# A hybrid decoder layer on one core: the mask of the forgetting attention moves from TensorE to GpSimd, its tiles run in the opposite order, and one product of the last expert turn changes places on VectorE

## The chip, the core and the metric

The kernel runs on one core of one Trainium2 chip. The core has five engines that take their instructions in order and wait for each other on semaphores: TensorE (PE, matrix products into PSUM), VectorE (DVE), ScalarE (ACT), GpSimd (POOL) and SyncE (SP, which here only issues DMAs). The metric is the device time of one execution in microseconds (us). Lower is better.

## The reference, cut to what matters

512 tokens of 1024 channels go through one layer: four token mixers with gates (a short convolution, a stick-breaking attention, a forgetting attention, a convolution module), then a mixture of 32 experts, then a final RMSNorm. Both attentions have four heads of 64 channels and are causal.

```python
# stick-breaking attention, per head
z = q @ k.T * scale
mask = kpos < qpos
log_not = where(mask, log_sigmoid(-z), 0)
after = reverse_cumsum(log_not) - log_not
out = where(mask, exp(log_sigmoid(z) + after), 0) @ v

# forgetting attention, per head; dcum is a running sum over the tokens of log forget gates
logits = q @ k.T * scale + dq[:, None] - dcum[None, :]
logits = where(kpos <= qpos, logits, -inf)
out = softmax(logits) @ v

# experts: each token takes two of 32
out += combine[:, e] * ((silu(t @ w_gate[e]) * (t @ w_up[e])) @ w_down[e])
```

## The kernel before

The program is written by hand, one instruction stream for each engine. The order of work is the order in which it is written; there is no scheduler. It has these stages, by the trace of before: eleven projections of the normalised input (to about 136 us), sixteen attention steps (144 to 295 us), the rest of the gates and branch products (to about 400 us), the output projection and the router, and then 17 expert turns to the end. Expert weights stream in by DMA through a ring of 21 buffers.

**The attention steps** (the tensor block's loop over `n in range(STEPS + 1)`, STEPS = 16, four steps for each head). One step does one tile of each attention:

- Of the stick-breaking attention, `stick_step(n)` gives key tile `kt = 3 - n % 4`. Its scores are keys x queries and cover the columns `q0:` = `kt * 128` to 512, so 128, 256, 384 and 512 columns in the four steps of a head.
- Of the forgetting attention, `fox_step(n)` gives query tile `qt = n % 4`. Its scores are queries x keys and cover the columns `0:m`, `m = (qt + 1) * 128`: also 128, 256, 384 and 512 columns. `fox_head` takes the other head of the same pair, which lies in the other 64 partitions.

In a step TensorE runs, in this order:

1. three pairs of score products, of the stick-breaking one into bank 0 (L1904) and the forgetting one into bank 1 (L1905). Both contract over 64 partitions, one in the lower and one in the upper half of the array's rows;
2. two 128x128 products that add a mask to the diagonal blocks: `identb` x `cutb` into bank 0 (L1906, after it `z_psum` is raised) and `identb` x `maskb` into bank 1 (L1908, after it `l_psum`);
3. 24 products of 512 columns for the gates (L1848, in the last steps L1873);
4. the running sums of the stick-breaking attention (L1915, L1918);
5. the products of weights and values of step n - 1: stick-breaking (L1927, output of 64 partitions and 512 - q0 columns, written before the other in the program) and forgetting (L1932, one product of 128 columns for each pair of key tile and query tile, so qt + 1 of them, output in the other 64 partitions). Both are plain float32 and appear in the trace as two records for each product;
6. the transposes of the forgetting weights (L1939, qt + 1 of them), and six branch products (L1860).

Meanwhile VectorE takes bank 0 (L1276, waits for `z_psum`), subtracts `dcum` from bank 1 with a running maximum (L1283, waits for `l_psum`, then raises `l_max`), and makes the split parts that TensorE's step 4 waits for (`spl`, L1108). ScalarE does the exponentials, among them `wts` (L958) and `pt` (L963), which step 5 of the next round waits for. GpSimd only adds up `run` (L694 to L697). `dcum`, the running sums broadcast to all partitions, has come by DMA before the first step.

**The last expert turn** (turn 16, `LAST`). TensorE multiplies the gate weights and then the up weights with the tokens (L2175), VectorE makes `hid` = gate and up product (L1105, raises `hid_r`), TensorE transposes it (L2184) and multiplies it with the down weights (L2201). While that goes on the results of the earlier turns, scattered to `y_dram`, are loaded back as four tiles of 128 tokens. `gather_results(1, tiles)` on VectorE waits until a tile has landed and adds its two weighted rows to the token (two instructions, L1105). Tile 1 (`EARLY_ROWS`) is loaded first; tiles 2 and 3 (`LATE_ROWS`) are weighted after the last turn, and TensorE takes tile 0. Then come the final norms and the stores.

VectorE's order in the last turn before:

```python
for j in range(2): dve.tensor_scalar(cw_diag[:, j, :], ...)
gather_results(1, EARLY_ROWS)
dve.wait_ge(S["silu"], E + 1)
dve.wait_ge(S["gu_done"], E + 1)
stt(hid[:, :], ...).then_inc(S["hid_r"], 1)
```

Of the kernel before, what the change touches and what calls it, by code (L numbers as in the profile page):

```python
# [48 lines left out]
def hybrid_trunk(nc, x, mix_norm_g, w_in, b_forget, conv_a_w, conf_dw_w, conf_dw_b, conf_ln_g,  # L49
                 conf_ln_b, w_branch, w_gate, b_gate, w_out, ffn_norm_g, w_router_group,  # L50
                 w_router_expert, w_expert_gate, w_expert_up, w_expert_down, final_norm_g, out):
    P = 128
# [50 lines left out]
    with main:  # L103
# [6 lines left out]
        def sem(name):  # L110
# [15 lines left out]
        rv = sb(main, "rv", [NT, 2, NE], F32R)  # L126
        neg_tri = sb(main, "neg_tri", [P], F32R)
        neg_one = sb(main, "neg_one", [P], F32R)
        maskb = sb(main, "maskb", [P], BF16)
        strictb = sb(main, "strictb", [P], BF16)  # L130
        oneb = sb(main, "oneb", [P], BF16)
        eps = sb(main, "eps", [1])
# [169 lines left out]


        S = {name: sem(name) for name in (
            "pool_step act_step dve_step consts small_in tabs_ready x0 x1 x2s x3 sq_done root xn_ready "
            "xt_psum hi_out xt_ready raw0 raw1 rest0 rest1 hi_ready split_ready unit_used "
            "tabs_psum free_p0 free_p1 "
            "ln_in ln_sum ln_cent ln_sq ln_root ln_norm ln_act y_ready ya ya_hi ya_split bf_in ff_step "
# [78 lines left out]
            return i // PER * PER + (i + 1) % PER  # L387

        def fox_step(n):
            return fox_head(n // NT), n % NT, (n % NT + 1) * P  # L390

        def x_tile(n):

# [251 lines left out]
        def _(pool):  # L645
# [5 lines left out]
                                          pattern=[[step, cols]], channel_multiplier=mult)  # L651

            for t, v in ((ident, 0.0), (causal, 1.0), (tri_made, -1.0), (one_made, -1.0),
                         (maskb, 0.0), (cutb, 0.0), (strictb, 1.0), (oneb, 1.0), (eps, EPS)):
                st.mark(pool.memset(t[:], v))
            st.mark(pool.memset(cu[:, :, 0:CF_W - 1], 0.0))
            st.mark(pool.memset(ca[:, :, 0:CA_W - 1], 0.0))
# [4 lines left out]
            st.mark(select(ident, P, ALU.not_equal, 1.0, 0, -1, 1))  # L662
            st.mark(select(causal, T, ALU.is_ge, 0.0, 0, 1, -1))
            st.mark(select(tri_made, P, ALU.is_ge, 0.0, 0, -1, 1))
            st.mark(select(maskb, P, ALU.is_ge, MASKED, 0, -1, 1))
            st.mark(select(cutb, P, ALU.is_gt, MASKED, 0, 1, -1))
            st.mark(select(strictb, P, ALU.is_gt, 0.0, 0, 1, -1))
            st.done()
            st.link(pool.tensor_copy(identb[:, :], ident[:, :]))
            pool.sem_inc(S["consts"], 1)  # L670

            evacuated(pool, "ac")
            evacuated(pool, "ab")
# [8 lines left out]
            for j in range(BJ):  # L682
                pool.wait_ge(S["ya_hi"], j + 1)
                pool.tensor_tensor(yl[0][:, j, :], axb[:, j, :], yh[0][:, j, :].bitcast(F32), ALU.subtract).then_inc(S["ya_split"], 1)

            for n in range(STEPS):
                h, kt, q0 = stick_step(n)
                if kt == 0:
                    continue
                pool.wait_ge(S["sp_max"], n + 1)  # L690
                if n:
                    pool.wait_ge(S["sp_lo"], parts(n))
                if kt == NT - 1:
                    pool.tensor_copy(run[:, q0:], sp[:, q0:]).then_inc(S["run_ready"], 1)  # L694
                else:
                    st.link(pool.tensor_copy(run[:, q0:q0 + P], sp[:, q0:q0 + P]))
                    pool.tensor_tensor(run[:, q0 + P:], run[:, q0 + P:], sp[:, q0 + P:], ALU.add).then_inc(S["run_ready"], 1)  # L697
# [96 lines left out]
        def _(act):  # L794
# [9 lines left out]
            for t in range(NT):  # L804
                act.wait_ge(x_in[t], 16)
                act.activation(junk[:, :], xt[:, t, :], ACT.Square, accum_out=stat[:, 0, t:t + 1]).then_inc(S["sq_done"], 1)
                act.wait_ge(S["sq_done"], t + 1)
                if t == 0:
                    act.wait_ge(S["consts"], 1)
                act.activation(stat[:, 1, t:t + 1], stat[:, 0, t:t + 1], ACT.Sqrt, bias=eps[:, 0:1], scale=1.0 / D).then_inc(S["root"], 1)  # L810

            def first_hi(part):
# [288 lines left out]
        def _(dve):  # L1101
# [75 lines left out]
                        st.mark(stt(sg[:, j, :], win, ch[:, j, CA_W + i:CA_W + i + 1], sg[:, j, :], ALU.mult, ALU.add))  # L1177

            split_lo(1, KC * PROJ[1][2])
            dve.wait_ge(S["consts"], 1)  # L1180
            st.mark(dve.tensor_copy(causal_r[:, :], causal[:, :]))
            st.mark(dve.tensor_copy(neg_tri[:, :], tri_made[:, :]))
            st.mark(dve.tensor_copy(neg_one[:, :], one_made[:, :]))
# [87 lines left out]
            for n in range(STEPS + 1):  # L1271
                if n < STEPS:

                    h, kt, q0 = stick_step(n)
                    dve.wait_ge(S["z_psum"], n + 1)
                    dve.tensor_scalar(tmp[:, q0:], bank[0][:, q0:], CAP, None, ALU.min).then_inc(S["sp_min"], 1)  # L1276

                    h, qt, m = fox_step(n)
                    sm = small[:, n % 2, :]
                    dve.wait_ge(S["l_psum"], n + 1)  # L1280
                    if n >= 1:
                        dve.wait_ge(S["pt_psum"], n)
                    st.link(dve.tensor_tensor_reduce(out=lg[:, 0:m], in0=bank[1][:, 0:m], in1=dcum[:, h, 0:m], scale=1.0,  # L1283
                                                     scalar=-3e38, op0=ALU.subtract, op1=ALU.max, accum_out=sm[:, 0:1]))
                    dve.sem_inc(S["l_max"], 1)

                    st.link(dve.tensor_tensor(sm[:, 1:2], sm[:, 0:1], dq[:, qt, h:h + 1], ALU.add))
                    dve.tensor_tensor(sm[:, 2:3], dq[:, qt, h:h + 1], sm[:, 1:2], ALU.subtract).then_inc(S["l_bias"], 1)

                    g, d = x_tile(n)  # L1290
                    b, c = gp[:, n % 2, :], gs[:, n % 2, :]
                    dve.wait_ge(S["xg_neg"], n + 1)
                    dve.tensor_scalar(b, c, CAP, None, ALU.min).then_inc(S["xg_min"], 1)
                    h, kt, q0 = stick_step(n)
                    dve.wait_ge(S["sp_ln"], n + 1)
                    if n:
                        dve.wait_ge(S["run_ready"], runs(n))
                    stt(sp[:, q0:], bank[0][:, q0:], 0.0, tmp[:, q0:], ALU.add, ALU.max).then_inc(S["sp_max"], 1)
                    dve.wait_ge(S["l_exp"], n + 1)
                    st.link(dve.reciprocal(sm[:, 4:5], sm[:, 3:4]))  # L1300
                    dve.tensor_scalar(lg[:, 0:m], lg[:, 0:m], sm[:, 4:5], None, ALU.mult).then_inc(S["l_norm"], 1)
                    dve.wait_ge(S["sp_hi"], parts(n) + 1)
                    if n:
                        dve.wait_ge(S["acc_done"], n)
                    lo(spl[:, q0:], sp[:, q0:], sph[:, q0:]).then_inc(S["sp_lo"], 1)
                    dve.wait_ge(S["xg_ln"], n + 1)
                    dve.tensor_tensor(b, b, c, ALU.max).then_inc(S["xg_max"], 1)
                    k, part = (n + 3) // 2, (n + 1) % 2
                    if n >= 1 and k <= NX:
                        x_lo_part(k, part)  # L1310

                    dve.wait_ge(S["xg_exp"], n + 1)
                    dve.wait_ge(S["xb_ps"], n + 1)
                    if g == 0:
                        dve.tensor_tensor(hsum[:, :, d, :], by_tile(c), by_tile(bank[4 + n % 2][:, :]), ALU.mult).then_inc(S["xg_free"], 1)
                    else:
                        dve.tensor_tensor(b, c, bank[4 + n % 2][:, :], ALU.mult).then_inc(S["xg_free"], 1)
                        dve.wait_ge(S["xg_free"], n + 1)
                        dve.tensor_tensor(hsum[:, :, d, :], hsum[:, :, d, :], by_tile(b), ALU.add)
                    if kt:  # L1320
                        dve.wait_ge(S["sp_hi"], parts(n) + 2)
                        lo(run_l[:, q0:], run[:, q0:], run_h[:, q0:]).then_inc(S["sp_lo"], 1)
                    if n == STEPS - 1:
                        gate_lo(1, 1)
# [288 lines left out]
            def expert_pass(c):  # L1613
# [16 lines left out]
                for i in range(turns):  # L1630
# [10 lines left out]
                    if isinstance(c, int) and i == LAST:  # L1641
                        dve.wait_ge(S["flag_ready"], 1)
                        most.append(dve.value_load(flag[0:1, 0:1], min_val=0, max_val=T))
                        for j in range(2):
                            dve.tensor_scalar(cw_diag[:, j, :], ident[:, :], cw[:, j, 0:1], None, ALU.mult).then_inc(S["comb"], 1)
                        gather_results(1, EARLY_ROWS)
                    dve.wait_ge(S["silu"], E + 1)
                    dve.wait_ge(S["gu_done"], E + 1)
                    stt(hid[:, :], bank[3][:, 0:FE], rslot[:, column(c, i)], act_g[:, :], ALU.mult, ALU.mult).then_inc(S["hid_r"], 1)
                    if i + 1 < turns:  # L1650
                        for b in range(2):
                            x_out(E + 1, b)
# [89 lines left out]
        def _(pe):  # L1742
# [9 lines left out]
            pe.wait_ge(S["dve_step"], 1)  # L1752
            for n in range(NIDLE):
                nc.tensor.matmul(bank[3][:, 0:P], pt[:, 0, :], pt[:, 1, :], start=True, stop=True)
            pe.wait_ge(S["consts"], 1)

            for t in range(NT):
                pe.wait_ge(S["xn_ready"], t + 1)
# [135 lines left out]
            for n in range(STEPS + 1):  # L1894
                if n < STEPS:
# [6 lines left out]
                    j2, r2 = head_rows(h)  # L1902
                    for i, (kz, qz, ql, kl) in enumerate(((k_s, q_s, q_f, k_f), (k_s, q_sl, q_f, k_fl), (k_sl, q_s, q_fl, k_f))):
                        nc.tensor.matmul(bank[0][:, q0:], kz[r:r + HD, j, kt * P:(kt + 1) * P], qz[r:r + HD, j, q0:], start=i == 0, stop=i == 2)  # L1904
                        nc.tensor.matmul(bank[1][:, 0:m], ql[r2:r2 + HD, j2, qt * P:(qt + 1) * P], kl[r2:r2 + HD, j2, 0:m], start=i == 0, stop=i == 2)  # L1905
                    nc.tensor.matmul(bank[0][:, q0:q0 + P], identb[:, :], cutb[:, :], start=False, stop=True,  # L1906
                                     skip_group_check=True).then_inc(S["z_psum"], 1)
                    nc.tensor.matmul(bank[1][:, m - P:m], identb[:, :], maskb[:, :], start=False, stop=True,  # L1908
                                     skip_group_check=True).then_inc(S["l_psum"], 1)
                    gates(BEHIND_SCORES)  # L1910
                if n < STEPS:
                    h, kt, q0 = stick_step(n)
# [336 lines left out]
```

## Time and profile before

| | |
|---|---|
| median of 3 runs | 710.95 us (710.42 to 713.12) |
| the profiled execution | 711.37 us, of it 709.5 us are the span of the profile |
| TensorE busy | 690.8 us (97%) |
| VectorE busy | 373.2 us (53%) |
| ScalarE busy | 254.5 us (36%) |
| GpSimd busy | 91.3 us (13%) |
| mean rate of the DMAs | 232 GB/s |
| chain that ended last | PE 89%, DVE 4%, DMA 3%, ACT 1% |

The span is the time from the first to the last record of the profile. Busy is the time in which at least one instruction of an engine ran. The last line follows the execution back from its last instruction, at each step to what released it. Matmuls overlap, their starts are recorded and their ends are modelled: the time that a group of them costs is read from start to start.

### The profile page before, as it was taken

The page shows a single profiled execution, that of the slowest core. Times are in us where ns is not written, and L with a number is a line of the kernel's source. Part 1 is how long each engine was busy: PE and PEld are TensorE (multiplying, and loading weights), DVE is VectorE, ACT ScalarE, POOL GpSimd, SP SyncE. Part 2 cuts the span into 40 slices and gives each one's busy share as a digit, 9 for nine tenths or more (in the row PEclk, how much of TensorE's full clock was granted, in tenths as well). Part 3 has the DMA queues.
Part 4 walks back from the last instruction along what each step waited for, and adds up shares of the span by engine and source line. Part 5 has one row for each costly group of instructions (what it writes and reads, how often), then busy time and mean ns, then how long its engine had stood idle before and what let it go on. Part 6 is the DMA issues. An engine that isn't in the chain of part 4 may idle for free.

```text
span 709.5 us, 10025 instructions
## 1 busy us (share of the span) xinstructions
PE 690.8 (97%) x3923; PEld 508.0 (72%) x3923; DVE 373.2 (53%) x732; ACT 254.5 (36%) x423; POOL 91.3 (13%) x130
## 2 busy tenths in 40 slices
PE   8999999999999999999999999999999999999894
PEld 7888988777777777788888888666555556555442
DVE  5378996666676868556446214752513121212227
ACT  7332133587676777544244211220101111111113
POOL 2000922000000101100003000011311312131100
PEclk9999999999999999999999999999999999999998
DMA  7523244322222111493406699699999999999993
GB/s 241 177 61 118 61 127 143 139 75 75 75 75 74 48 59 49 162 385 113 136 2 237 225 382 346 268 353 387 405 417 420 403 419 418 419 419 417 419 394 134
DMA packets 60585, 164.58 MB, mean 232 GB/s; under 512 B 8090, under 2 KB 39911, under 8 KB 48116
## 3 DMA queue, kind: packets, MB, share of 16 engines
q1 hardware_dynamic: 54820, 151.77, 56.3%
q0 software_dynamic: 5712, 12.11, 4.6%
q8 instruction: 33, 0.54, 0.3%
q14 instruction: 20, 0.16, 0.1%
HBM read 155.68 MB, written 16.00 MB: 242 GB/s over the span
## 4 chain that ended last, share of the span: by engine, by line
PE 89%; DVE 4%; DMA 3%; ACT 1%; issue 1%; POOL 0%; SPq 0%; POOLq 0%; DVEq 0%; ACTq 0%
PE psum L1749 31%; PE psum L2175 14%; PE psum L1848 12%; PE psum L2201 8%; PE psum L2028 6%; PE psum L1860 3%; PE psum L2141 2%; DVE ring_e L1105 2%; DMA ring_e<-y_dram 2%; PE psum L1873 1%; PE psum L1904 1%; PE psum L2184 1%; DMA y_dram<-ye,slots_b 1%; PE psum L1987 1%; PE psum L1939 1%
## 5 line engine op out<-in xcount | busy, mean ns | idle before, releaser
L1749 PE MATMUL psum<-xh,wh 128*128 128x512 f32 x256 | 99.9, 390 | 0.8 <-DVE xl L1105 0.8
L1749 PE MATMUL psum<-xl,wh 128*128 128x512 f32 x256 | 99.6, 389 | 0.0
L1749 PE MATMUL psum<-xh,wl 128*128 128x512 f32 x256 | 99.6, 389 | 0.0
L1108 DVE TENSOR_TENSOR wl<-raw,wh 128x1280 fp32r<-128x1280 f32 (+4 forms) x37 | 71.8, 1945 | 24.6 <-ACT wh L801 9.0
L1105 DVE SCALAR_TENSOR_TENSOR hid<-psum,rslot,act_g 128x256 f32<-128x256 f32 x17 | 8.2, 483 | 92.3 <-PE psum L2175 91.7
L1749 PEld LDWEIGHTS psum<-xh,wh 128*128 128x128 f32 x256 | 48.1, 188 | 11.0 <-DVE xl L1105 1.0
L1749 PEld LDWEIGHTS psum<-xh,wl 128*128 128x128 f32 x256 | 48.1, 188 | 10.0
L1749 PEld LDWEIGHTS psum<-xl,wh 128*128 128x128 f32 x256 | 48.1, 188 | 9.8
L1848 PE MATMUL psum<-xh,wh 128*128 128x512 f32 x128 | 51.3, 401 | 0.0
L1848 PE MATMUL psum<-xh,wl 128*128 128x512 f32 x128 | 50.1, 391 | 0.0
L1848 PE MATMUL psum<-xl,wh 128*128 128x512 f32 x128 | 49.9, 390 | 0.0
L1105 DVE SCALAR_TENSOR_TENSOR sg<-cu,ch,sg 128x512 f32<-128x512 f32 x60 | 48.7, 882 | 0.0
L2175 PE MATMUL psum<-ring_w,xT 128*64 128x256 f32 x256 | 38.8, 383 | 0.0
L1054 ACT ACTIVATE act_g<-psum,rslot 128x256 f32<-128x256 f32 x17 | 8.0, 473 | 77.7 <-PE psum L2175 49.3
L1056 ACT ACTIVATE hidT<-psum 128x256 f32<-128x256 f32 x17 | 6.5, 383 | 78.2 <-PE psum L2184 78.2
L1670 DVE COPY ye<-psum 128x512 f32<-128x512 f32 x15 | 10.4, 691 | 44.2 <-PE psum L2201 44.2
L739 POOL DMA_INDIRECT y_dram<-ye,slots x15 | 13.7, 913 | 143.8 <-DVE ye L1670 125.4
L1335 DVE TENSOR_TENSOR gp<-gs,psum 128x512 f32<-128x512 f32 x16 | 11.0, 685 | 36.8 <-PE psum L1749 36.0
L2175 PEld LDWEIGHTS psum<-ring_w,xT 128*64 128x64 f32 x256 | 22.3, 136 | 10.5 <-issue 3.4
L976 ACT ACTIVATE gs<-psum,bg 128x512 f32<-128x512 f32 x16 | 10.9, 687 | 50.2 <-PE psum L1749 50.2
L1848 PEld LDWEIGHTS psum<-xh,wl 128*128 128x128 f32 x128 | 24.0, 188 | 5.2
L1848 PEld LDWEIGHTS psum<-xl,wh 128*128 128x128 f32 x128 | 24.1, 188 | 4.6
(388 smaller groups left out, 1531.6 us busy)
## 6 DMA issues: line engine op xcount, KB each, us to landing
raw<-in_w_gate SPq DMA_DIRECT2D x16, 1024.0 KB, 6.3
raw<-in_w_in SPq DMA_DIRECT2D x9, 1024.0 KB, 5.5
ring_w<-in_w_expert_gate SPq DMA_DIRECT2D x8, 1024.0 KB
ring_w<-in_w_expert_up SPq DMA_DIRECT2D x8, 1024.0 KB
ring_h<-in_w_expert_down SPq DMA_DIRECT2D x8, 1024.0 KB
ring_h<-in_w_expert_gate SPq DMA_DIRECT2D x6, 1024.0 KB
ring_e<-in_w_expert_down SPq DMA_DIRECT2D x6, 1024.0 KB
ring_e<-in_w_expert_gate SPq DMA_DIRECT2D x6, 1024.0 KB
```

Source lines behind the costliest of these rows:

```text
L739: pool.indirect_dma_start(out=y_dram[:, :], out_offset=bass.IndirectOffsetOnAxis(ap=slots[first, p], axis=0), in_=ye[first, :], in_offset= ...
L976: act.activation(gs[:, m, :], gate_bank(cg, m)[:, :], ACT.Sigmoid, bias=bg[:, d:d + 1]).then_inc(S["gate_mul"], 1)
L1105: return dve.scalar_tensor_tensor(out=out_, in0=a, scalar=s, in1=b, op0=o0, op1=o1)
L1108: return dve.tensor_tensor(dst, src, hi.bitcast(F32), ALU.subtract)
L1335: dve.tensor_tensor(gp[:, m, :], gs[:, m, :], branch_bank(cg, m)[:, :], ALU.mult).then_inc(S["gate_free"], 1)
L1749: last = nc.tensor.matmul(dst, a, b, start=start and n == 0, stop=stop and n == len(seq) - 1)
L1848: last = nc.tensor.matmul(bank[6 + n % 2][:, :], a[:, c, f], b[:, c, :], start=c == 0 and q == 0, stop=c == KC - 1 and q == 2)
L1860: last = nc.tensor.matmul(bank[4 + n % 2][:, :], a[:, j, f], b[g][:, j, :], start=j == 0 and q == 0, stop=j == BJ - 1 and q == 2)
L2028: last = nc.tensor.matmul(bank[t][:, :], x_[:, t, c, :], w_[:, b, c, :], start=c == 0 and m == 0, stop=c == KC - 1 and m == 2)
L2141: last = nc.tensor.transpose(bank[b][:, (k % 4) * P:(k % 4 + 1) * P], xg[:, s, :].rearrange("p (n c) -> p c n", c=KC)[:, k, :], ident[:, :])
L2175: last = nc.tensor.matmul(dst[half, 0:FE], xT[:, k, half], w[h][:, k, :], start=k == 0, stop=k == KC - 1)
L2201: last = nc.tensor.matmul(bank[5 + b][half, :], hidT[:, m, half], w_d[h][:, m, b * T:(b + 1) * T], start=m == 0, stop=m == FE // P - 1)
```

## The change

There are two parts, and each one moves something.

**The mask.** `maskb`, its memset, its select and TensorE's sixteen products with it (L1908) are gone. GpSimd writes the mask into `dcum` itself: `later_keys(n)` selects over the 128 columns of the diagonal block of head h and puts +2^100 where the key lies after the query, so that VectorE's subtraction (L1283) gives the masked logit. One block of `dcum` is read by all later query tiles too, so the mask may only go in when they are done: `fox_step` now takes the query tiles from the last to the first (`qt = 3 - n % 4`, so m = 512, 384, 256, 128 in the steps of a head), and GpSimd masks the block of step n + 1 after VectorE has raised `l_max` for step n. VectorE waits for this mask (`made`) ahead of L1283. `l_psum` is now raised by the last score product, ahead of L1906.

**The last turn.** `gather_results(1, EARLY_ROWS)` goes behind the product `hid`.

```diff
@@
         def fox_step(n):
-            return fox_head(n // NT), n % NT, (n % NT + 1) * P
+            qt = NT - 1 - n % NT
+            return fox_head(n // NT), qt, (qt + 1) * P
@@ gpsimd, constants
             for t, v in ((ident, 0.0), (causal, 1.0), (tri_made, -1.0), (one_made, -1.0),
-                         (maskb, 0.0), (cutb, 0.0), (strictb, 1.0), (oneb, 1.0), (eps, EPS)):
+                         (cutb, 0.0), (strictb, 1.0), (oneb, 1.0), (eps, EPS)):
...
-            st.mark(select(maskb, P, ALU.is_ge, MASKED, 0, -1, 1))
...
-            pool.sem_inc(S["consts"], 1)
+            pool.sem_inc(S["made"], 1)
@@ gpsimd, attention
+            def later_keys(n):
+
+                h, qt, m = fox_step(n)
+                select(dcum, P, ALU.is_ge, -MASKED, 0, -1, 1, dcum[:, h, m - P:m]).then_inc(S["made"], 1)
+
+            pool.wait_ge(S["dc_in"], 16)
+            later_keys(0)
             for n in range(STEPS):
                 h, kt, q0 = stick_step(n)
+                if n + 1 < STEPS:
+                    pool.wait_ge(S["l_max"], n + 1)
+                    later_keys(n + 1)
                 if kt == 0:
                     continue
                 pool.wait_ge(S["sp_max"], n + 1)
@@ vector, attention
                     if n >= 1:
                         dve.wait_ge(S["pt_psum"], n)
+                    dve.wait_ge(S["made"], n + 2)
                     st.link(dve.tensor_tensor_reduce(out=lg[:, 0:m], in0=bank[1][:, 0:m], in1=dcum[:, h, 0:m], ...
@@ vector, expert turns
                         for j in range(2):
                             dve.tensor_scalar(cw_diag[:, j, :], ident[:, :], cw[:, j, 0:1], None, ALU.mult).then_inc(S["comb"], 1)
-                        gather_results(1, EARLY_ROWS)
                     dve.wait_ge(S["silu"], E + 1)
                     dve.wait_ge(S["gu_done"], E + 1)
                     stt(hid[:, :], bank[3][:, 0:FE], rslot[:, column(c, i)], act_g[:, :], ALU.mult, ALU.mult).then_inc(S["hid_r"], 1)
+                    if isinstance(c, int) and i == LAST:
+                        gather_results(1, EARLY_ROWS)
@@ tensor, attention
-                        nc.tensor.matmul(bank[1][:, 0:m], ql[...], kl[...], start=i == 0, stop=i == 2)
+                        last = nc.tensor.matmul(bank[1][:, 0:m], ql[...], kl[...], start=i == 0, stop=i == 2)
+                    last.then_inc(S["l_psum"], 1)
                     nc.tensor.matmul(bank[0][:, q0:q0 + P], identb[:, :], cutb[:, :], start=False, stop=True,
                                      skip_group_check=True).then_inc(S["z_psum"], 1)
-                    nc.tensor.matmul(bank[1][:, m - P:m], identb[:, :], maskb[:, :], start=False, stop=True,
-                                     skip_group_check=True).then_inc(S["l_psum"], 1)
```

The waits for `consts` on the three other engines are waits for the first count of `made` now, and the tile `maskb` is no longer allocated.

## Rows read from the trace of the kernel before

**Rows 1.** Chain that ended last, 140 to 300 us, shares by line

```profile
by line: PE psum L1848 53.9%; PE psum L1860 13.9%; PE psum L1873 6.2%; PE psum L1904 6.1%; PE psum L1939 3.8%; PE psum L1927 3.7%; PE psum L1932 3.4%; PE psum L1915 3.0%; PE psum L1918 1.9%; PE psum L1906 1.6%; issue 0.7%; PE psum L1908 0.6
```

**Rows 2.** Waits of PE, 125 to 300 us: total us, times, longest

```profile
PE psum L1927 <- ACT pt L963: 0.2, 1, 0.2
```

**Rows 3.** Timeline of PE, score blocks of four steps: start us, us, what

```profile
152.28 0.38 PE L1904 MATMUL psum<-q_s,k_s 64*128 64x256 f32 x1
...
152.84 0.23 PE L1906 MATMUL psum<-cutb,identb 128*128 128x128 bf16 x1
...
161.14 0.44 PE L1904 MATMUL psum<-q_s,k_s 64*128 64x384 f32 x1
...
161.86 0.23 PE L1906 MATMUL psum<-cutb,identb 128*128 128x128 bf16 x1
...
170.64 0.50 PE L1904 MATMUL psum<-q_s,k_s 64*128 64x512 f32 x1
170.65 0.50 PE L1905 MATMUL psum<-k_f,q_f 64*128 64x512 f32 x1
...
171.54 0.23 PE L1906 MATMUL psum<-cutb,identb 128*128 128x128 bf16 x1
171.61 0.22 PE L1908 MATMUL psum<-maskb,identb 128*128 128x128 bf16 x1
...
180.89 0.32 PE L1904 MATMUL psum<-q_s,k_s 64*128 64x128 f32 x1
...
181.37 0.23 PE L1906 MATMUL psum<-cutb,identb 128*128 128x128 bf16 x1
```

**Rows 4.** Timeline of PE, weights-and-values blocks, narrowest and widest

```profile
159.01 0.32 PE L1927 MATMUL psum<-wts,sv 128*64 128x128 f32 x1
...
159.38 0.44 PE L1939 MATMUL psum<-ident,lg 128*128 128x128 f32 x2
...
187.31 0.64 PE L1927 MATMUL psum<-wts,sv 128*64 128x512 f32 x1
187.31 0.65 PE L1932 MATMUL psum<-pt,fv 128*64 128x128 f32 x4
187.78 0.59 PE L1927 MATMUL psum<-wts,sv 128*64 128x512 f32 x1
...
188.33 0.33 PE L1939 MATMUL psum<-ident,lg 128*128 128x128 f32 x1
```

**Rows 5.** Timeline of PE, turn 8: only one half of the array's columns

```profile
576.18 3.62 PE L2175 MATMUL psum<-ring_y,xT 128*64 128x256 f32 x16
```

**Rows 6.** Timeline of DVE and PE, widest step: split part, its use

```profile
175.25 0.69 DVE L1108 TENSOR_TENSOR spl<-sp,sph 128x512 fp32r<-128x512 f32 x1
177.21 0.39 PE L1915 MATMUL psum<-sph,neg_tri 128*128 128x512 f32 x1
```

**Rows 7.** Timeline of POOL: a select over 128 columns of float32

```profile
3.83 0.28 POOL L650 TENSOR_SCALAR_AFFINE_SELECT tri_made<-tri_made 128x128 f32<-128x128 f32 x1
```

**Rows 8.** Timeline of ACT and PE at the end of the attention steps

```profile
293.55 0.59 ACT L963 ACTIVATE pt<-psum 128x512 f32<-128x512 f32 x1
294.19 0.64 PE L1927 MATMUL psum<-wts,sv 128*64 128x512 f32 x1 [0.25 <-ACT pt L963]
```

**Rows 9.** Timeline of PE and DVE, last turn and what follows

```profile
679.08 3.67 PE L2175 MATMUL psum<-ring_w,xT 128*64 128x256 f32 x32
681.21 1.29 DVE L1105 SCALAR_TENSOR_TENSOR ring_e<-ring_e,cw,x 128x1024 f32<-128x1024 f32 x1 [6.45 <-DMA ring_e<-y_dram]
683.86 0.48 DVE L1105 SCALAR_TENSOR_TENSOR hid<-psum,rslot,act_g 128x256 f32<-128x256 f32 x1
691.77 1.27 DVE L1105 SCALAR_TENSOR_TENSOR ring_e<-ring_e,cw,x 128x1024 f32<-128x1024 f32 x1
```

**Rows 10.** Second load of tile 2: its issue, and KB and us to landing

```profile
671.75 1.52 SPq L606 DMA_DIRECT2D ring_e<-y_dram  x1
ring_e<-y_dram SPq DMA_DIRECT2D x1, 512.0 KB, 19.5
```

More of the change, by code:

```diff
@@ L128, in hybrid_trunk @@
         neg_one = sb(main, "neg_one", [P], F32R)
-        maskb = sb(main, "maskb", [P], BF16)
         strictb = sb(main, "strictb", [P], BF16)
@@ L304, in hybrid_trunk @@
         S = {name: sem(name) for name in (
-            "pool_step act_step dve_step consts small_in tabs_ready x0 x1 x2s x3 sq_done root xn_ready "
+            "pool_step act_step dve_step made small_in tabs_ready x0 x1 x2s x3 sq_done root xn_ready "
             "xt_psum hi_out xt_ready raw0 raw1 rest0 rest1 hi_ready split_ready unit_used "
@@ L808, in _ @@
                 if t == 0:
-                    act.wait_ge(S["consts"], 1)
+                    act.wait_ge(S["made"], 1)
                 act.activation(stat[:, 1, t:t + 1], stat[:, 0, t:t + 1], ACT.Sqrt, bias=eps[:, 0:1], scale=1.0 / D).then_inc(S["root"], 1)
@@ L1179, in _ @@
             split_lo(1, KC * PROJ[1][2])
-            dve.wait_ge(S["consts"], 1)
+            dve.wait_ge(S["made"], 1)
             st.mark(dve.tensor_copy(causal_r[:, :], causal[:, :]))
@@ L1754, in _ @@
                 nc.tensor.matmul(bank[3][:, 0:P], pt[:, 0, :], pt[:, 1, :], start=True, stop=True)
-            pe.wait_ge(S["consts"], 1)
+            pe.wait_ge(S["made"], 1)
             for t in range(NT):
@@ L1904, in _ @@
                         nc.tensor.matmul(bank[0][:, q0:], kz[r:r + HD, j, kt * P:(kt + 1) * P], qz[r:r + HD, j, q0:], start=i == 0, stop=i == 2)
-                        nc.tensor.matmul(bank[1][:, 0:m], ql[r2:r2 + HD, j2, qt * P:(qt + 1) * P], kl[r2:r2 + HD, j2, 0:m], start=i == 0, stop=i == 2)
+                        last = nc.tensor.matmul(bank[1][:, 0:m], ql[r2:r2 + HD, j2, qt * P:(qt + 1) * P], kl[r2:r2 + HD, j2, 0:m], start=i == 0, stop=i == 2)
+                    last.then_inc(S["l_psum"], 1)
                     nc.tensor.matmul(bank[0][:, q0:q0 + P], identb[:, :], cutb[:, :], start=False, stop=True,
                                      skip_group_check=True).then_inc(S["z_psum"], 1)
-                    nc.tensor.matmul(bank[1][:, m - P:m], identb[:, :], maskb[:, :], start=False, stop=True,
-                                     skip_group_check=True).then_inc(S["l_psum"], 1)
                     gates(BEHIND_SCORES)
```

## The prediction, made before the changed kernel ran

> **What bounds the kernel now.** I looked first at the busy shares in the table above: TensorE works in 97% of the span. So the question for each edit is what it does to TensorE's own list of work, and only then whether it makes a wait. The chain that ended last, taken over the attention steps, says the same: it is made of PE lines nearly throughout, more than half of it the gate products of L1848 [rows 1]. The table of waits over that stretch has a single entry for PE, 0.2 us [rows 2]. The sixteen steps are therefore bound by the number and length of TensorE's products. The other engines have room: in the widest step, where both attentions work on 512 columns, VectorE ends the split part at 175.94 us (175.25 + 0.69) and TensorE takes it at 177.21, 1.27 us later [rows 6].
>
> The end of the kernel is another matter. In the last turn the up product starts at 679.08 and takes 3.67 us, to 682.75, but `hid` starts at 683.86, since VectorE first weights the early tile, which landed just before 681.21 [rows 9]. From 691.77 on VectorE weights the late tiles and runs without a pause into the final norms, so there it is VectorE's queue and the tiles' landings that set the end.
>
> **The products with the mask.** From L1906 to L1908 TensorE needs 0.07 us (171.54 to 171.61) [rows 3]. Sixteen such products are removed, and the chain confirms that they lie on the path, if only with 0.6% of its 160 us [rows 1]: 16 x 0.07 = **1.1 us** gained. The chain's share alone would be 0.9 us, and I keep 0.9 to 1.3 for the range.
>
> **What takes their place on GpSimd.** A select over 128 columns of float32 takes 0.28 us [rows 7]. The select for step n + 1 starts after the maximum of step n and is wanted some 9 us later (successive steps start at 161.14, 170.64 and 180.89 [rows 3]). The only work queued behind it on GpSimd is the copy and sum of `run`, which first waits for a later VectorE instruction. I cost it at nothing; what hides it is the whole TensorE step, and without that cover it would be 0.28 us in each of 16 steps, 4.5 us.
>
> **The new order of the tiles.** This is a part that the title of the change does not name, and it is on TensorE's path. Before, both attentions had the same width in each step. The two score products of a pair use different halves of the array's rows and run at the same time: L1904 and L1905 with 512 columns start at 170.64 and 170.65 [rows 3]. The same holds for weights and values, which use different halves of the columns: the records of L1927 and L1932 both start at 187.31 [rows 4]. That one half alone is no faster than two shows in turn 8, where 16 records of L2175 on one half take 3.62 us [rows 5], while 32 on both halves take 3.67 us [rows 9]. So a block costs what its wider half costs.
>
> Now the widths no longer match: the steps of a head pair 128 with 512, 256 with 384, 384 with 256 and 512 with 128 columns. The cost of a block by width, start to start:
>
> - Scores, from L1904 to L1906 [rows 3]: 0.48 us for 128 columns (180.89 to 181.37), 0.56 for 256, 0.72 for 384, 0.90 for 512. A head cost 0.48 + 0.56 + 0.72 + 0.90 = 2.66 and will cost 0.90 + 0.72 + 0.72 + 0.90 = 3.24. That is 0.58 more, times four heads **2.3 us**.
> - Weights and values, from L1927 to L1939 [rows 4]: 0.37 us for 128 columns (159.01 to 159.38) and 1.02 for 512 (187.31 to 188.33), so (1.02 - 0.37) / 3 = 0.22 for each 128 more. A head had the widths 1, 2, 3, 4 in units of 128, ten units, and will have 4, 3, 3, 4, fourteen. Four units more at 0.22 make 0.87, times four heads **3.5 us**.
>
> The transposes of the forgetting weights are as many as before (4 + 3 + 2 + 1), only in another step, and the columns of the stick-breaking sums do not change. On VectorE and ScalarE the load becomes even: no step has both widths at 512, so none of their chains is longer than the one that had 1.27 us to spare [rows 6]. The first step is the exception that I checked: VectorE comes to it late, and the forgetting tile is now 512 wide there. That lengthens the chains of both engines, but TensorE also arrives later, by the 0.42 us of its wider score block, so I take no wait there; it is the first place to look for one.
>
> On this point the Trainium skill has a rule that would make the change dearer. Two records of the values block speak about it: a second L1927 starts at 187.78, after the first L1932 of 187.31, though the program has both of L1927's passes ahead of L1932 [rows 4]. "TensorE: Matmul & The Clock Gate", Part 3, "The mechanism", says that matmuls start and end strictly in program order; "TensorEngine Tiling (Array Packing)", "Key Properties", says that different tiles run independently. By that strict order the forgetting part would begin only with the second pass of the other; the trace speaks for the independent tiles. What the strict order would cost is the third rival below.
>
> **The end of the attention steps.** TensorE waits there for the last `pt`, which ScalarE ends at 294.14 (293.55 + 0.59); the block starts at 294.19 [rows 8]. In the last step the forgetting tile is 128 wide now, so `pt` ends sooner by about 0.3 us and the work ahead of it on both engines shrinks as well; TensorE's own list ahead of it has three transposes fewer, which is counted above as moved. Bounds: nothing, and the 0.3 us. I take **0.1 us** gained, nearer to nothing because a copy of 2560 columns stays ahead of `wts` on ScalarE.
>
> **The last turn.** `hid` can start when the up product is done, at about 682.8 in place of 683.86: 1.1 us earlier, and the transposes and down product with it [rows 9]. The two weightings of tile 1 take 2 x 1.3 us and fall into the time in which VectorE waited for the down product, so nothing is queued behind them that is wanted sooner. But VectorE then wants tile 2 at 691.77 - 1.1 = 690.7, and the second load of that tile, issued at 671.75, landed 19.5 us later, at 691.25 [rows 10]. The loads depend on scatters and weight buffers that were done before `hid`, so they don't come earlier. The gain is cut to 691.77 - 691.25 = **0.5 us**, and the wait for the early tile becomes one for tile 2. Bounds: nothing (if the landing varies by half a microsecond) and 1.1.
>
> **The start.** GpSimd saves a memset and a select before it releases the other engines. ScalarE is the first that asks, after the first token tile has come by DMA; I cost it at nothing.
>
> **The sum.** -1.1 + 2.3 + 3.5 - 0.1 - 0.5 = **+4.1 us**. Everything after the attention steps follows TensorE: the expert weights are first loaded after those steps and after the last branch products, so a later end of the steps moves the DMAs by the same time and is not caught up. The profiled execution took 711.37 us and would take 715.5. It lies 0.4 us above the median of the runs, 710.95, so the prediction is 710.95 + 4.1 = **715.0 us**, 0.6% slower.
>
> **Rivals.**
>
> 1. *The wider half does not bind* (0.15). If TensorE could go on with the next work on the free half, or begin the gate products while the wider half still runs, a block would cost the mean of its two widths. Each step then has 640 columns, the same 2560 a head as before, and the +5.8 vanish: 715.0 - 5.8 = 709.2 us, not slower. For it speaks only that the columns in total don't grow. Against it: L1906 and L1915 use all rows, L1939 all columns, and turn 8 shows that an idle half gives nothing back [rows 5]. It decides from the point where more than 2.3 us of the 5.8 are hidden, for then the change is within 0.5%; half of them hidden gives 712.1.
> 2. *The mask comes late* (0.03). GpSimd's select would then delay L1283 and, through `pt` and `wts`, TensorE. With nothing hidden it is 4.5 us more, 719.5. Against it: 9 us of cover.
> 3. *The values block runs in strict order* (0.09). Then the narrow stick-breaking product must be through one or both passes before the wide one starts. With the 0.22 us of a unit, half of it a pass, and 0.15 fixed, the four blocks of a head cost about 1.13, 1.02, 0.92 and 1.02, together 4.1 in place of 3.6: 0.45 x 4 = 1.8 us more, 716.8.
> 4. *The end gives the full 1.1 us or nothing* (0.08): 714.4 or 715.5.
>
> **How the numbers follow.** The forecast has 0.65. Its own range is the sum of its bounds: mask products 0.9 to 1.3, end of the steps 0 to 0.3, last turn 0 to 1.1, blocks read to about 0.3 us, so 714.0 to 716.0. The wide range goes down to 712.7, which takes in the first rival with up to 40% of the 5.8 hidden, and up to 717.0 for the third; outside remain about 0.10 below and 0.03 above. Half a per cent, 3.55 us, is about what a measurement of this kernel can tell from no change, and it lies at 714.5, close under the forecast. Slower by more than that: four fifths of the forecast, rivals 2 and 3 and half of rival 4, 0.52 + 0.03 + 0.09 + 0.03 = 0.67. Faster by over 0.5% (under 707.4) would need rival 1 in full and more: 0.03. The rest, 0.30, is within.
>
> **What would show it.** In the profile after: no L1908 and sixteen more selects on GpSimd; the score blocks of a head at 0.90, 0.72, 0.72, 0.90 us and the values blocks at 1.02, 0.80, 0.80, 1.02; a head of steps 1.2 us longer than before; no new PE wait in that stretch; `hid` right behind the up product; VectorE waiting a few tenths for tile 2. The prediction is wrong if the unequal blocks cost less than the wider half, if a PE wait appears on `wts`, `pt` or `lg` in the first step, or if the loads at the end come sooner.

## The result, and the profile after

| | before | changed |
|---|---|---|
| median | 711.11 us (7 runs, 709.54 to 713.12) | 715.52 us (7 runs, 713.63 to 717.70) |
| ratio | | 1.0055, 95% interval 1.0034 to 1.0076 |
| the profiled execution | 711.37 us, span 709.5 | 715.26 us, span 713.5 |

The change makes the kernel slower by 0.55%. The forecast was 715.0 us and 0.6%; the range was 712.7 to 717.0. The profiled executions lie 3.9 us apart, their spans 4.0.

The first line of the page is the busy time of the engines, their share of the span and their instructions:

```profile
PE 694.7 (97%) x3907; PEld 507.4 (71%) x3907; DVE 373.8 (52%) x732; ACT 254.1 (36%) x423; POOL 96.1 (13%) x144
```

TensorE has sixteen products less (3907 for 3923) and is busy 3.9 us longer. VectorE and ScalarE have not moved. So the lost time is TensorE's own work and not a new wait in the attention steps; waits in the last turns, told below, change the total by under 1 us.

The score blocks in the timeline of PE, the first two steps of the first head. They answer to [rows 3]; L1904, L1905 and L1906 are L1915, L1916 and L1918 now:

```profile
144.44 0.32 PE L1915 MATMUL psum<-q_s,k_s 64*128 64x128 f32 x1
144.44 0.49 PE L1916 MATMUL psum<-k_f,q_f 64*128 64x512 f32 x1
144.60 0.27 PE L1915 MATMUL psum<-q_sl,k_s 64*128 64x128 f32 x1
144.71 0.27 PE L1915 MATMUL psum<-q_s,k_sl 64*128 64x128 f32 x1
144.77 0.39 PE L1916 MATMUL psum<-k_fl,q_f 64*128 64x512 f32 x1
145.01 0.39 PE L1916 MATMUL psum<-k_f,q_fl 64*128 64x512 f32 x1
145.33 0.23 PE L1918 MATMUL psum<-cutb,identb 128*128 128x128 bf16 x1
...
150.93 0.22 PE L1925 MATMUL psum<-sph,neg_tri 128*128 128x128 f32 x1
...
153.04 0.38 PE L1915 MATMUL psum<-q_s,k_s 64*128 64x256 f32 x1
153.04 0.44 PE L1916 MATMUL psum<-k_f,q_f 64*128 64x384 f32 x1
...
153.77 0.23 PE L1918 MATMUL psum<-cutb,identb 128*128 128x128 bf16 x1
```

The 128 columns and the 512 columns start together at 144.44. The narrow ones are through by their third record at 144.71, and L1918, which needs all rows of the array, waits for the wide ones until 145.33. The block takes 0.89 us where the equal pair of 128 took 0.48. The pair 256 and 384 takes 0.73 (153.04 to 153.77).

The blocks of weights and values of steps 1 and 4, which answer to [rows 4] (L1927, L1932 and L1939 are L1937, L1942 and L1949 now):

```profile
159.87 0.32 PE L1937 MATMUL psum<-wts,sv 128*64 128x128 f32 x1
159.88 0.32 PE L1942 MATMUL psum<-pt,fv 128*64 128x128 f32 x1
160.03 0.27 PE L1937 MATMUL psum<-wts,sv 128*64 128x128 f32 x1
160.04 0.93 PE L1942 MATMUL psum<-pt,fv 128*64 128x128 f32 x7
160.89 0.55 PE L1949 MATMUL psum<-ident,lg 128*128 128x128 f32 x3
...
188.97 0.64 PE L1937 MATMUL psum<-wts,sv 128*64 128x512 f32 x1
188.97 0.43 PE L1942 MATMUL psum<-pt,fv 128*64 128x128 f32 x2
189.45 0.59 PE L1937 MATMUL psum<-wts,sv 128*64 128x512 f32 x1
189.97 0.66 PE L1949 MATMUL psum<-ident,lg 128*128 128x128 f32 x4
```

Whichever side is the wide one, the block takes within 0.02 us what 512 columns took before: 1.02 us (159.87 to 160.89) and 1.00 us (188.97 to 189.97). The width of the other side makes no difference beyond that. The forecast was 1.02.

Waits of PE from 125 to 306 us (total us, times, longest) have one entry, as in [rows 2]:

```profile
PE psum L1937 <- ACT pt L972: 0.2, 1, 0.2
```

The mask on GpSimd, in the timeline of POOL:

```profile
155.13 0.29 POOL L650 TENSOR_SCALAR_AFFINE_SELECT dcum<-dcum 128x128 f32<-128x128 f32 x1 [5.44 <-DVEq L1295]
156.17 0.29 POOL L705 COPY run<-sp 128x128 f32<-128x128 f32 x1 [0.74 <-DVE sp L1114]
```

The select takes 0.29 us, and GpSimd still waits 0.74 us for VectorE before the sum of `run`. It is hidden, as forecast.

**The last turn**, timelines of DVE and PE, with the issue of tile 2's second load and its landing. They answer to [rows 9, 10]:

```profile
683.46 3.67 PE L2185 MATMUL psum<-ring_w,xT 128*64 128x256 f32 x32
...
687.25 0.48 DVE L1114 SCALAR_TENSOR_TENSOR hid<-psum,rslot,act_g 128x256 f32<-128x256 f32 x1 [8.09 <-PE psum L2185]
687.65 1.28 DVE L1114 SCALAR_TENSOR_TENSOR ring_e<-ring_e,cw,x 128x1024 f32<-128x1024 f32 x1
...
690.69 1.51 PE L2211 MATMUL psum<-ring_h,hidT 128*64 128x512 f32 x6 [0.55 <-DMA ring_h<-in_w_expert_down]
...
695.77 1.28 DVE L1114 SCALAR_TENSOR_TENSOR ring_e<-ring_e,cw,x 128x1024 f32<-128x1024 f32 x1
...
677.27 0.44 SPq L606 DMA_DIRECT2D ring_e<-y_dram  x1
ring_e<-y_dram SPq DMA_DIRECT2D x1, 512.0 KB, 18.3
```

The down product of the last turn before, in the timeline of PE:

```profile
686.68 3.65 PE L2201 MATMUL psum<-ring_h,hidT 128*64 128x512 f32 x16
```

Up to the down product of turn 14 the changed kernel is 4.9 us late (the first record of L2211 is at 659.53; the first of L2201 before was at 654.62). In turn 15 TensorE waits for an up weight, 1.38 us before and 0.89 in the changed kernel, and by the up product of the last turn the lateness is 4.4 us (683.46 and 679.08). This wait varies between profiles: with the old order of the tiles it lies between 0.35 and 1.38 us, and in that of experiment 3, which does nothing new up to there, it is 0.99. With the new order it is 0.18 to 0.89 in three profiles; that the later end of the attention steps shortens it is not shown. In the last turn `hid` gains its 1.0 us: it is 3.4 us later than before (687.25 and 683.86). But TensorE then waits 0.55 us for the last down weights, and from there to the end all is 4.0 us later (690.69 and 686.68). Tile 2 lands at 695.57 (677.27 + 18.3), 0.2 us before VectorE takes it at 695.77.

### The profile page after: what moved, and what is told of

Its sections match the earlier page's. It is cut to its first block, busy times and chain, and to the rows that moved or that the text cites. A ratio compares the mean times of both kernels' runs of the same rounds, so it can differ in the third digit from the quotient of the medians.

```text
span 713.5 us, 10024 instructions
## 1 busy us (share of the span) xinstructions
PE 694.7 (97%) x3907; PEld 507.4 (71%) x3907; DVE 373.8 (52%) x732; ACT 254.1 (36%) x423; POOL 96.1 (13%) x144
## 4 chain that ended last, share of the span: by engine, by line
PE 89%; DVE 4%; DMA 4%; ACT 1%; issue 1%; SPq 0%; POOL 0%; POOLq 0%; DVEq 0%; ACTq 0%
PE psum L1760 31%; PE psum L2185 14%; PE psum L1859 12%; PE psum L2211 8%; PE psum L2038 6%; PE psum L1871 3%; PE psum L2151 2%; DMA ring_h<-in_w_expert_down 2%; DVE ring_e L1114 1%; PE psum L1884 1%; PE psum L1937 1%; DMA y_dram<-ye,slots_b 1%; PE psum L1915 1%; PE psum L2194 1%; PE psum L1997 1%
## 5 line engine op out<-in xcount | busy, mean ns | idle before, releaser
L1760 PEld LDWEIGHTS psum<-xh,wh 128*128 128x128 f32 x256 | 48.1, 188 | 11.1 <-DVE xl L1114 1.0
L1760 PEld LDWEIGHTS psum<-xl,wh 128*128 128x128 f32 x256 | 48.1, 188 | 9.7
L1859 PEld LDWEIGHTS psum<-xh,wh 128*128 128x128 f32 x128 | 24.2, 189 | 4.5
```

Of the source, the lines that this page charges most:

```text
L1760: last = nc.tensor.matmul(dst, a, b, start=start and n == 0, stop=stop and n == len(seq) - 1)
L1859: last = nc.tensor.matmul(bank[6 + n % 2][:, :], a[:, c, f], b[:, c, :], start=c == 0 and q == 0, stop=c == KC - 1 and q == 2)
```

## The experiments

Each is timed against the kernel before, and its times are compared with those of before on the same chip.

Beside the times, the traces give one length that can be compared between all of them: from the first score product of the first step to the last block of weights and values.

| | from, to (us) | length (us) | against before |
|---|---|---|---|
| before | 144.35, 294.19 | 149.84 | |
| changed | 144.44, 299.06 | 154.62 | +4.78 |
| 1, the order alone | 144.52, 299.92 | 155.40 | +5.56 |
| 2, mask and last turn, old order | 144.35, 293.35 | 149.00 | -0.84 |
| 3, the last turn alone | 144.43, 294.27 | 149.84 | 0.00 |
| 4, mask put back, old order | 144.63, 293.64 | 149.01 | -0.83 |
| 7, one side made narrow | 144.23, 293.90 | 149.67 | -0.17 |
| 8, the mask alone | 144.97, 293.98 | 149.01 | -0.83 |

These are single profiles, but the kernels with the same products on TensorE in these steps (before and 3; 2, 4 and 8) agree within 0.01 us, so the length tells smaller differences than the medians do.

**1. The order alone.** The kernel before with this edit:

```diff
-            return fox_head(n // NT), n % NT, (n % NT + 1) * P
+            qt = NT - 1 - n % NT
+            return fox_head(n // NT), qt, (qt + 1) * P
```

> The kernel before with nothing changed but the order of the forgetting attention's query tiles (the mask stays two products on TensorE, the early tile is still weighted ahead of hid). Theory A, a block costs what its wider half costs: 5.8 us more in the attention steps and 0.1 less at their end, about 716.8 us (ratio 1.008), score blocks of a head 0.90, 0.72, 0.72, 0.90 us. Theory B, the columns in total set the cost, and the extra time of the changed kernel came from GpSimd's mask or its waits: no change here, 711.1 us.

Measured: 716.65 us, before 710.82, ratio 1.0078 (1.0065 to 1.0091), that is 5.5 us more by the ratio. In its timeline of PE the block of step 1 is the one of the changed kernel:

```profile
160.05 0.32 PE L1928 MATMUL psum<-wts,sv 128*64 128x128 f32 x1
...
161.07 0.55 PE L1940 MATMUL psum<-ident,lg 128*128 128x128 f32 x3
```

That is 1.02 us for 128 columns beside 512, and the attention steps are 5.56 us longer. Theory A holds, and theory B, in which GpSimd or the total of columns is to blame, is out: GpSimd does nothing new here and the total is unchanged.

**2. The mask and the last turn, with the old order.** The changed kernel with the edit above taken back.

> The changed kernel with the old order of the query tiles, so that both attentions have equal widths again. GpSimd masks each block in place, so the later query tiles of a head read masked keys: that part of the forgetting attention is not the reference's. Theory A: the mask products' 1.1 us and the last turn's 0.5 to 1.0 us are gained and nothing is paid, about 709.3 us (ratio 0.9975 against before). Theory B, that GpSimd's mask costs the time: still about 715 us.

Measured: 709.69 us, before 710.82, ratio 0.9978 (0.9969 to 0.9987), 1.6 us less. The same block in its timeline of PE:

```profile
158.88 0.32 PE L1936 MATMUL psum<-wts,sv 128*64 128x128 f32 x1
...
159.25 0.44 PE L1948 MATMUL psum<-ident,lg 128*128 128x128 f32 x2
```

It is 0.37 us again. The mask on GpSimd is not what costs time, and without the order the change is a small gain. This kernel leaves out part of the work of a right one (the later query tiles of a head read masked keys); experiment 4 puts that right.

**3. The last turn alone.** The kernel before with this edit:

```diff
                         for j in range(2):
                             dve.tensor_scalar(cw_diag[:, j, :], ...)
-                        gather_results(1, EARLY_ROWS)
                     dve.wait_ge(S["silu"], E + 1)
                     dve.wait_ge(S["gu_done"], E + 1)
                     stt(hid[:, :], ...)
+                    if isinstance(c, int) and i == LAST:
+                        gather_results(1, EARLY_ROWS)
```

> The kernel before with the early tile's weightings behind hid and nothing else. hid starts 1.0 us earlier. Theory A (what lands last sets the end): the gain is cut to about 0.5 us, 710.6 us, and the profile shows a wait of TensorE for the last down weights or of VectorE for tile 2. Theory C (VectorE's queue alone set it): the full 1.0 us, 710.1 us.

Measured: 711.19 us, before 710.82, ratio 1.0005 (0.9991 to 1.0019): no difference that can be told, from 0.6 us less to 1.4 more. Its timeline of PE shows the wait for the down weights:

```profile
683.06 0.51 PE L2185 MATMUL psum<-ident,hid 128*128 128x128 f32 x2 [0.66 <-DVE hid L1105]
685.97 1.51 PE L2202 MATMUL psum<-ring_h,hidT 128*64 128x512 f32 x6 [0.56 <-DMA ring_h<-in_w_expert_down]
```

In this one profile the down product starts 0.7 us sooner than before (685.97 and 686.68), and its span is 708.8 for 709.5. But 0.35 us of that is there before `hid`: the up product starts at 678.73 and started at 679.08. So the last turn itself is 0.4 us shorter. The interval includes the 0.5 us that theory A gave and not the 1.0 of theory C.

**4. The mask on GpSimd, right, with the old order.** GpSimd saves the block, masks it, and puts it back when the maximum has been taken. The saved block of 128 columns has no room of its own; it takes the place of two constants of the router (`strictb`, `oneb`), which GpSimd now makes after the attention steps, with a wait of TensorE for them.

```diff
             def later_keys(n):
                 h, qt, m = fox_step(n)
-                select(dcum, P, ALU.is_ge, -MASKED, 0, -1, 1, dcum[:, h, m - P:m]).then_inc(S["made"], 1)
+                block = dcum[:, h, m - P:m]
+                if qt:
+                    st.link(pool.tensor_copy(dcum[:, h, m - 2 * P:m - P], keys[:, :]))
+                if qt < NT - 1:
+                    st.link(pool.tensor_copy(keys[:, :], block))
+                select(dcum, P, ALU.is_ge, -MASKED, 0, -1, 1, block).then_inc(S["made"], 1)
```

> The changed kernel with the old order, and right for every tile: GpSimd saves the diagonal block of dcum, masks it, and puts the saved block back once the maximum of that step is taken. Two copies more for each step on GpSimd, some 0.9 us of work in a step of 9 us. Theory A: all of it is hidden, about 709.3 us (ratio 0.9975), like the kernel with the mask and the old order. Theory D, GpSimd's longer list delays the sums of run and through them TensorE: a wait of PE appears in the attention steps and the time is 711 us or more.

Measured: 709.85 us, before 710.82, ratio 0.9982 (0.9972 to 0.9993), 1.3 us less. PE has one wait in the attention steps, 0.3 us for the last `pt`. The timeline of POOL in a step:

```profile
163.44 0.29 POOL L691 COPY dcum<-keys 128x128 f32<-128x128 f32 x1 [7.05 <-DVEq L1304]
163.88 0.29 POOL L652 TENSOR_SCALAR_AFFINE_SELECT dcum<-dcum 128x128 f32<-128x128 f32 x1
164.98 0.29 POOL L711 COPY run<-sp 128x128 f32<-128x128 f32 x1 [0.81 <-DVE sp L1123]
```

GpSimd puts the block back, masks the next one, and waits another 0.81 us for VectorE. In this step it copies once; where it copies twice the wait is down to 0.23 us, so the cover is there but thin:

```profile
154.22 0.29 POOL L691 COPY dcum<-keys 128x128 f32<-128x128 f32 x1 [4.51 <-DVEq L1304]
154.57 0.30 POOL L693 COPY keys<-dcum 128x128 f32<-128x128 f32 x1
155.02 0.29 POOL L652 TENSOR_SCALAR_AFFINE_SELECT dcum<-dcum 128x128 f32<-128x128 f32 x1
155.55 0.29 POOL L711 COPY run<-sp 128x128 f32<-128x128 f32 x1 [0.23 <-DVE sp L1123]
```

Theory D is out. This version is faster than both kernels, than before by 0.2 per cent.

**5. The down weights ahead of the scatters.** The changed kernel with this edit on SyncE:

```diff
+            for w in last_down:
+                wait_reuse(0, w)
+                load_unit_no(w, 0, found)
             for s in range(2):
                 sp_e.wait_ge(scattered[s], ...)
             load_results(EARLY_ROWS)
-            for w in last_down:
-                wait_reuse(0, w)
-                load_unit_no(w, 0, found)
```

> The changed kernel with one move in the DMA queue: the last turn's two down weights are asked for ahead of the wait for the scatters and of the early tile's load, so they land before hid is transposed. In the profile of the changed kernel TensorE waits 0.6 us for them. Theory A (several landings lie close together, and the next one takes over): that wait is gone, the early tile lands later, and tile 2, which landed 0.2 us before VectorE took it, sets the end; 0.2 us or nothing is gained, about 715.3 us. Theory E (the down weights alone took the last turn's gain): the 0.6 us come back, about 714.9 us.

Measured: 715.08 us, before 710.92, ratio 1.0054 (1.0038 to 1.0070), no different from the changed kernel's 1.0055. In its timeline of DVE:

```profile
687.27 0.48 DVE L1114 SCALAR_TENSOR_TENSOR hid<-psum,rslot,act_g 128x256 f32<-128x256 f32 x1 [8.10 <-PE psum L2185]
690.42 1.28 DVE L1114 SCALAR_TENSOR_TENSOR ring_e<-ring_e,cw,x 128x1024 f32<-128x1024 f32 x1 [2.67 <-DMA ring_e<-y_dram]
...
695.44 1.28 DVE L1114 SCALAR_TENSOR_TENSOR ring_e<-ring_e,cw,x 128x1024 f32<-128x1024 f32 x1 [0.18 <-DMA ring_e<-y_dram]
```

TensorE's wait for the down weights is gone from the profile. But the early tile lands just before 690.42, where in the changed kernel it had landed at 685.5 (issued at 674.43, 11.1 us). Its weightings start 2.8 us later (690.42 and 687.65), and VectorE then waits 0.18 us for tile 2, as theory A has it. Tile 2 is taken 0.33 us sooner than in the changed kernel. The down product starts 0.6 us sooner (690.09 and 690.69), and about half of this reaches the late tiles. The times can't tell the two theories' 715.3 and 714.9 apart, and the 0.33 us lies between their 0.2 and 0.6; what speaks for theory A is the wait for tile 2.

**6. Both together.** Kernel 4 with the edit of 5.

> The kernel that puts the keys back, in the old order, with the same move of the down weights in the DMA queue. Theory A: as without the move, about 709.8 us. Theory E: 0.6 us less, about 709.2 us.

Measured: 709.83 us, before 710.92, ratio 0.9982 (0.9973 to 0.9991). That is theory A's figure, but the interval also holds theory E's 709.2 (ratio 0.9976). Its timelines decide:

```profile
678.76 3.67 PE L2195 MATMUL psum<-ring_w,xT 128*64 128x256 f32 x32
...
685.38 3.65 PE L2221 MATMUL psum<-ring_h,hidT 128*64 128x512 f32 x16
...
690.95 1.28 DVE L1123 SCALAR_TENSOR_TENSOR ring_e<-ring_e,cw,x 128x1024 f32<-128x1024 f32 x1 [0.40 <-DMA ring_e<-y_dram]
```

TensorE no longer waits for the down weights, and VectorE waits 0.40 us for tile 2. From the up product to the late tiles it is 12.19 us (678.76 to 690.95), where the changed kernel took 12.31 (683.46 to 695.77): the move gives 0.1 us here, not 0.6.

**7. One side made narrow.** The kernel before with this edit:

```diff
-                    for kt in range(qt + 1):
+                    for kt in (qt,):
                         last = nc.tensor.matmul(bank[3][...], fv[:, kt, ...], pt[:, kt, :],
-                                                start=kt == 0, stop=kt == qt)
+                                                start=True, stop=kt == qt)
```

> The kernel before with the forgetting attention's weights and values product cut to its diagonal key tile, one product of 128 columns in each step in place of one to four; the other key tiles are left out of the sum. The stick-breaking product beside it stays 128 to 512 columns wide. Theory A, a block costs what its wider half costs: the blocks stay at 0.37, 0.59, 0.80, 1.02 us and the time at 711.0 us, though 24 products are gone. Theory B, the columns in total set the cost: 3 units of 128 columns less for each head at 0.22 us, 2.6 us less, 708.3 us.

Measured: 710.89 us, before 710.92, ratio 1.0005 (0.9989 to 1.0021). The block in its timeline of PE that stands beside the last one of [rows 4]:

```profile
187.13 0.64 PE L1927 MATMUL psum<-wts,sv 128*64 128x512 f32 x1
187.13 0.43 PE L1932 MATMUL psum<-pt,fv 128*64 128x128 f32 x2
187.61 0.59 PE L1927 MATMUL psum<-wts,sv 128*64 128x512 f32 x1
188.13 0.33 PE L1939 MATMUL psum<-ident,lg 128*128 128x128 f32 x1
```

It takes 1.00 us with one forgetting product and took 1.02 with four. For the 24 products that are gone only 0.17 us comes back in all of the attention steps together. Theory B's 2.6 us would be a ratio of 0.9963, far outside the interval.

**8. The mask alone.** Kernel 4 with the early tile's weightings ahead of `hid` again.

> The kernel that puts the keys back, in the old order, with the early tile's weightings ahead of hid as before: the mask on GpSimd alone. Theory A: the mask products' 1.1 us and nothing of the last turn, 709.9 us (ratio 0.9985), which is the same within the noise as with the weightings moved, since that move alone showed no gain. Theory D, the mask products cost nothing on TensorE: 711 us.

Measured: 710.19 us, before 710.92, ratio 0.9986 (0.9975 to 0.9996), 1.0 us less, with 0.3 to 1.8 in the interval. The attention steps are 0.83 us shorter in its trace. The mask products did lie on the path, and theory D is out. With the weightings moved, kernel 4 gave 0.9982; these intervals can't tell them apart.

## Why the prediction was right

- **TensorE's list decides in the attention steps.** Right: its one wait there stayed at 0.2 us, and all of the loss lies in the length of its blocks.
- **The mask products, 1.1 us.** From L1918 to the first running sum it is 5.60 us (145.33 to 150.93), and it was 5.67 from L1906 (171.54 to 177.21 [rows 3, 6]; 5.66 in other steps). So a product gave back 0.06 to 0.07 us, 1.0 to 1.1 in all. In experiments 2, 4 and 8 the attention steps are only 0.8 us shorter; 0.1 of the difference is TensorE's last wait for `pt`, 0.34 us in these traces where it was 0.25. In the times experiment 8 shows 1.0 us.
- **The new order, 2.3 + 3.5 us.** Score blocks of the first head: 0.89, 0.73, 0.73, 0.89 us for the 0.90, 0.72, 0.72, 0.90 forecast. Values blocks: 1.02, 0.81, 0.79, 1.00 for 1.02, 0.80, 0.80, 1.02. A head went from 37.67 us (180.89 to 218.56) to 38.88 (182.19 to 221.07), 1.2 us as forecast. Experiment 1 measures the order alone at 5.5 us by the times and 5.56 in the trace, where 5.7 was the sum with the end of the steps. That an idle half gives nothing back was read from turn 8 and is shown directly by experiment 7.
- **Rival 1, the columns in total.** Out by experiments 1 and 7. The prediction says that this rival decides from 2.3 us hidden. That is where the time would leave the range (715.0 - 2.3 = 712.7); half a per cent lies at 714.5, so 0.5 us hidden would have been enough to come within it.
- **Rival 2, the mask comes late.** Out: no wait for it, and experiment 4 puts one or two more copies of 0.29 us on GpSimd in each step without a loss.
- **Rival 3, the strict order.** Out: the block with 128 columns of `wts` beside 512 took 1.02 us, not 1.13. The second L1937 starts after the first L1942 (160.03 and 159.88), as in [rows 4]. In step 4 it is plainer: both records of L1942, which stands behind L1937 in the program, lie between 188.97 and 189.40, and the second of L1937 starts at 189.45. On this kernel the trace agrees with the Trainium skill's "TensorEngine Tiling (Array Packing)", "Key Properties", by which tiles run independently. The strict program order that its page "TensorE: Matmul & The Clock Gate", Part 3, "The mechanism", states does not hold between the two halves here.
- **Rival 4, the end gives the full 1.1 us or nothing.** The full gain is out by experiment 3, whose interval ends at 0.6 us less. Nothing at all can't be excluded by the times; the profiles show 0.4.
- **The end of the attention steps, 0.1 us.** From the last transpose to the last block it is 1.90 us (297.16 to 299.06) and was 2.29 (291.90 to 294.19). The three transposes fewer account for 0.33 of it, 0.06 are left, near the 0.1 forecast.
- **The first step.** No wait appeared.
- **The last turn, 0.5 us.** The size is about right in the profile, 0.4 us, and the timing cannot show it (experiment 3). The reason given was wrong for this kernel. The prediction had VectorE wait for tile 2; it did not. TensorE's wait for the last down weights came first and took 0.55 us of the 1.0; I had not looked at that transfer, whose landing the profile of before did not give. Only when it is moved ahead (experiments 5 and 6) does VectorE wait for tile 2. That the figure came out is luck: tile 2 landed 0.2 us before it was taken, so its landing would have allowed 0.6 us where the down weights allowed 0.4.
- **The sum.** +4.1 us forecast, +4.0 in the spans, +4.4 between the medians. That the spans agree to 0.1 us is in part chance: the attention steps gave +4.8 where 4.6 was forecast, the start came 0.1 us later, the last turn gave 0.4 back, and the other 0.5 is the wait for the up weight in turn 15, which no term had and which differs between profiles. The medians, which are not tied to one such wait, lie 4.4 us apart, where 4.8 + 0.1 - 0.4 is 4.5. The parts of the times agree within their intervals: 5.5 (experiment 1) less 1.6 (experiment 2) is 3.9.

## What to carry to other kernels

When two narrow products share TensorE's array, look at how their widths are paired before you change the order of a loop: in these blocks the wider one set the cost, so an order that balances the work of the other engines can unbalance the pairs. An in-place edit that forces such an order can be bought back with a save and a restore on an idle engine. Where several transfers land close together, removing one wait shows the next, and only what is left after the last of them is a gain.

## What the runs showed of the hardware that was not expected

The two records of one float32 product and those of its neighbour on the other half run side by side even where one side has eight records and the other two: in step 1 seven records of L1942 follow from 160.04 on after the second one of L1937 has started at 160.03. In the last turn the transfers from `y_dram`, 512 KB each, took long to land (tile 2's second load 18.3 us in the changed kernel and 19.5 before [rows 10]) while the weights were still coming in, and asking for 2 MB of weights ahead of them (experiment 5) made the early tile land 4.9 us later.
